# One 512-column matmul for the high and the low part of x in four stages of a two-block network

## The chip, the cores and the metric

The kernel runs on one core of one Trainium2 chip. The metric is the device time of one execution in microseconds (us). TensorE (PE in the profile) multiplies; VectorE (DVE), ScalarE (ACT) and GpSimd (POOL) work on vectors; SyncE (SP) issues the weight transfers. A difference is told apart from no change here when it is over 0.2%.

## The reference, cut to what matters

The program runs two blocks one after the other on x of 256 tokens by 2048 features, each block two layers deep.

```python
for i in range(DEPTH):                       # first block, layers 0 and 1
    h = rmsnorm(x, g_pre[i])
    u, z = split(h @ w_in[i])                # 4096 columns each
    y = pool_mixer(u, ...) if i == 0 else rglru(causal_depthwise_conv(u, ...), ...)
    y = y * silu(z)
    o = y @ w_out[i]
    x = x + rmsnorm(o, g_post[i])
    gate = sigmoid(rmsnorm(x, g_ple_in[i]) @ w_ple_gate[i])
    x = x + rmsnorm((p[i] @ w_ple[i]) * gate, g_ple_out[i])
for l in range(DEPTH):                       # second block, layers 2 and 3
    h = rms_norm(x, norm_g); proj = h @ w_in # attention, spatial gate and gated linear attention
    merged = g0 * (y_a @ w_branch[0]) + g1 * (y_b @ w_branch[1]) + g2 * (y_c @ w_branch[2])
    x = x + merged @ w_out
```

All of it is in float32.

## The kernel before

**Three products for one.** Each weight and each activation is kept as two fp32r numbers, a high part and a low part. A product is `w_hi*x_hi + w_hi*x_lo + w_lo*x_hi`; the term of both low parts is left out. Activations are stored as `[128, features/128, 512]` with the 256 tokens' high parts in columns 0 to 255 and their low parts in columns 256 to 511 (`xs`, `inner`, `latent`, `y_abc`, `merged`).

**Units.** Weights come as 1144 units of 8 tiles of 128x128. SP loads unit n into one of 4 slots of `raw`, ACT rounds it to `w_hi` (L1058), DVE subtracts to get `w_lo` (L1528), PE uses both. `LOOKAHEAD` is 3 units. A slot is free again when PE has finished the unit that was in it (`pe_mark`).

**Stages.** A stage is a number of turns over a few output tiles ("products") of a given depth. In the order of the program: window, pooled, silu, squared, plain, gate (layer 0); conv, lru, squared, plain, gate (layer 1); then for layers 2 and 3 gqk to za, twelve pairs mix_gate and mix_branch, and wo. The stages that this change speaks of are these:

- pooled: 4 turns of 8 products, depth 8 tiles, from `inner`; DVE takes each product out of its PSUM bank with bias and scale (L1971).
- silu: 8 turns of 4 products, depth 16, from `xs`; DVE multiplies with the norm's factor (L1978), ACT makes tanh (L1432), DVE finishes (L2050, L2056), POOL splits the result into `inner` (L2269, L2270).
- squared, in layers 0 and 1: 4 turns of 4 products, depth 32, from `inner`; ACT takes each product out twice, scaled (L1394) and squared (L1396), POOL adds the squares up (L2380).
- wo, in layers 2 and 3: 4 turns of 4 products, depth 16, from `merged`; DVE adds half of the product to `x_buf` (L2012).

In `products`, PE goes through a unit's 8 tiles twice: first two matmuls per tile with `w_hi`, on x's columns 0 to 255 (L591) and 256 to 511 (L592), both added into the same 256 columns of the bank, then one per tile with `w_lo` on columns 0 to 255 (L602). `first_turn` does the same for stages that go by rows of the weight matrix in their first turn (L732, L734, L754): here layer 1's squared and both wo. Each matmul loads its 128x128 stationary tile itself.

In the stages that go by token (gv, vb, uv, mix_gate, mix_branch; `token_products`), x is the stationary operand and the weights are the moving one, 512 columns at a time (L650 with `w_hi`, L667 with `w_lo`). There the moving operand is read through `four_runs`: runs of 4 numbers (16 bytes), each run 64 bytes after the last, 32 of them, and that four times over. The output is written straight through.

**What sets the order.** Every engine's instructions are in program order; semaphores tie them. PE waits for `hi_done` and `lo_done` of a unit, for the reader of what stood in a bank before (`occupant`, `read_of`), and in a stage's first turn for the tiles of its operand. pooled and silu rotate over 4 banks, squared over 7. ACT and DVE do a unit's split first and the evictions (`events`) of that unit after it. `SETTLED` and `settle` place pairs of 128-column matmuls (L612) whose result nothing reads. `xs_offset` is an unused buffer of 448 bytes that sets where `xs` and all behind it lie.

## Time and profile before

| | us |
|---|---|
| median of 3 runs | 3226.94 (3226.93 to 3227.39) |
| the profiled execution | 3227.28 |
| its span in the trace | 3225.4 |
| PE busy in the span | 3219.8 |
| DVE busy | 2248.8 |
| ACT busy | 1675.2 |

The span runs from the first to the last instruction of the trace; 1.9 us of the profiled execution lie outside of it. A matmul's "mean ns" in the trace is its latency, of which most lies under the matmuls before and after it; the time that one really takes of PE is the distance from start to start. The granted clock is 1.00 for the whole span.

### The profile page before, as it was taken

How to read it: one execution, taken by the hardware profiler on the slowest of the kernel's cores; microseconds unless marked ns; L12 is line 12 of the kernel's file. 1: busy time of each engine (PE TensorE's matmuls, PEld its weight loads, DVE VectorE, ACT ScalarE, POOL GpSimd, SP SyncE). 2: the span in 40 equal slices, each digit the busy share in tenths (PEclk: the TensorE clock that was granted, in tenths of full speed). 3: DMA queues.
4: the chain of work that ended last, by engine and by line, in shares of the span. 5: the costliest groups of instructions: out<-in, count | busy, mean ns of one | idle time of the engine just before them, and what ended most of it. 6: DMA issues, size and time to landing. Idle time of an engine off the chain costs nothing.

```text
span 3225.4 us, 57779 instructions
## 1 busy us (share of the span) xinstructions
PE 3219.8 (100%) x24078; PEld 3063.7 (95%) x24078; DVE 2248.8 (70%) x2898; ACT 1675.2 (52%) x2084; POOL 742.3 (23%) x782
## 2 busy tenths in 40 slices
PE   9999999999999999999999999999999999999999
PEld 9999999999999999999899988889999999888889
DVE  7986654588888844887889755555668897555554
ACT  5344444565588844655655544444455545444443
POOL 2632320054644400332523200000014332000000
PEclk9999999999999999999999999999999999999999
DMA  7565665556665665556455566666665554665665
GB/s 248 184 203 191 196 226 192 180 191 210 196 194 192 197 224 195 188 186 205 163 181 180 171 200 196 196 196 196 194 195 180 180 176 161 197 198 196 196 198 174
DMA packets 172596, 622.71 MB, mean 193 GB/s; under 512 B 19632, under 2 KB 22704, under 8 KB 171952
## 3 DMA queue, kind: packets, MB, share of 16 engines
q1 hardware_dynamic: 165888, 601.96, 57.5%
q10 hardware_dynamic: 6160, 16.02, 1.4%
q8 instruction: 190, 3.11, 0.4%
q0 software_dynamic: 288, 1.05, 0.1%
q14 instruction: 70, 0.57, 0.1%
HBM read 611.61 MB, written 5.24 MB: 191 GB/s over the span
## 4 chain that ended last, share of the span: by engine, by line
PE 99%; DVE 1%; DMA 0%; ACT 0%; issue 0%; ACTq 0%; DVEq 0%
PE banks L650 20%; PE banks L602 13%; PE banks L591 13%; PE banks L592 13%; PE banks L667 10%; PE pm L602 5%; PE pm L592 5%; PE pm L591 5%; PE banks L754 2%; PE banks L732 2%; PE banks L734 2%; PE pm L754 2%; PE pm L734 2%; PE pm L732 2%; PE pm L926 0%; PE pm L802 0%
## 5 line engine op out<-in xcount | busy, mean ns | idle before, releaser
L1528 DVE TENSOR_TENSOR w_lo<-raw,w_hi 128x1024 fp32r<-128x1024 f32 x1144 | 1471.0, 1291 | 855.6 <-ACT w_hi L1058 849.2
L1058 ACT ACTIVATE w_hi<-raw 128x1024 fp32r<-128x1024 f32 x1143 | 1203.8, 1058 | 1094.3 <-PE banks L667 460.2
L591 PE MATMUL banks<-xs,w_hi 128*128 128x256 f32 x2468 | 577.9, 277 | 0.2 <-DVE taps_in L2017 0.2
L592 PE MATMUL banks<-xs,w_hi 128*128 128x256 f32 x2468 | 576.6, 276 | 0.0
L650 PE MATMUL banks<-w_hi,xs 128*128 128x512 f32 x2048 | 493.5, 381 | 0.0
L591 PEld LDWEIGHTS banks<-xs,w_hi 128*128 128x128 f32 x2468 | 463.4, 188 | 0.7 <-DVE taps_in L2017 0.4
L592 PEld LDWEIGHTS banks<-xs,w_hi 128*128 128x128 f32 x2468 | 463.5, 188 | 0.3
L650 PEld LDWEIGHTS banks<-w_hi,xs 128*128 128x128 f32 x2048 | 383.8, 188 | 68.1
L602 PE MATMUL banks<-xs,w_lo 128*128 128x256 f32 x2468 | 338.1, 278 | 0.0
L602 PEld LDWEIGHTS banks<-xs,w_lo 128*128 128x128 f32 x2468 | 305.2, 188 | 3.6 <-issue 3.3
L667 PE MATMUL banks<-w_lo,xs 128*128 128x512 f32 x1024 | 270.6, 384 | 0.0
L591 PE MATMUL pm<-xs,w_hi 128*128 128x256 f32 x956 | 223.3, 276 | 0.0
L592 PE MATMUL pm<-xs,w_hi 128*128 128x256 f32 x956 | 223.3, 276 | 0.0
L667 PEld LDWEIGHTS banks<-w_lo,xs 128*128 128x128 f32 x1024 | 190.2, 188 | 32.6
L592 PE MATMUL banks<-inner,w_hi 128*128 128x256 f32 x896 | 211.0, 276 | 0.0
L591 PE MATMUL banks<-inner,w_hi 128*128 128x256 f32 x896 | 211.0, 276 | 0.0
L650 PE MATMUL banks<-w_hi,y_abc 128*128 128x512 f32 x768 | 184.3, 380 | 0.0
L591 PEld LDWEIGHTS pm<-xs,w_hi 128*128 128x128 f32 x956 | 179.5, 188 | 0.0
L592 PEld LDWEIGHTS pm<-xs,w_hi 128*128 128x128 f32 x956 | 179.5, 188 | 0.0
L592 PEld LDWEIGHTS banks<-inner,w_hi 128*128 128x128 f32 x896 | 168.2, 188 | 0.0
L591 PEld LDWEIGHTS banks<-inner,w_hi 128*128 128x128 f32 x896 | 168.2, 188 | 0.0
L650 PEld LDWEIGHTS banks<-w_hi,y_abc 128*128 128x128 f32 x768 | 144.1, 188 | 24.8
(411 smaller groups left out, 5428.6 us busy)
## 6 DMA issues: line engine op xcount, KB each, us to landing
raw<-weights SPq DMA_DIRECT2D x1143, 512.0 KB, 3.5
wide<-x_in ACTq DMA_DIRECT2D x1, 2048.0 KB, 8.7
x_scratch<-wide ACTq DMA_DIRECT2D x1, 2048.0 KB, 11.1
wide<-x_scratch ACTq DMA_DIRECT2D x1, 2048.0 KB, 8.9
wide<-x_in ACTq DMA_DIRECT2D x3, 512.0 KB, 6.8
out_x<-wide SPq DMA_DIRECT2D x3, 512.0 KB, 5.3
g_v<-x_scratch ACTq DMA_DIRECT2D x2, 512.0 KB, 4.9
w_st<-w_s ACTq DMA_DIRECT2D x2, 512.0 KB, 4.6
```

The lines of the kernel that those rows point to most:

```text
L591: nc.tensor.matmul(bank, w_hi[:, slot, w], x[:, 0:T], start=(k + t == 0), stop=False)
L592: nc.tensor.matmul(bank, w_hi[:, slot, w], x[:, T:2 * T], start=False, stop=False)
L602: ins = nc.tensor.matmul(bank, w_lo[:, slot, w], p.operand(i, k + t)[:, 0:T], start=False, stop=(k + t == p.depth - 1))
L650: nc.tensor.matmul(product_bank(s, i, j), x[:, at:at + P], four_runs(w_hi[:, slot, w]), start=(k == 0 and at < T), stop=False)
L667: ins = nc.tensor.matmul(product_bank(s, i, j), x[:, j * P:(j + 1) * P], four_runs(w_lo[:, slot, w]), start=False, stop=(k == depth - 1))
L732: nc.tensor.matmul(bank, w_hi[:, slot, w], operand[:, k, 0:T], start=(k == 0 and j < 4), stop=False, skip_group_check=True)
L734: nc.tensor.matmul(bank, w_hi[:, slot, w], operand[:, k, T:2 * T], start=False, stop=False, skip_group_check=True)
L754: ins = nc.tensor.matmul(bank, w_lo[:, slot, w], operand[:, k, 0:T], start=False, stop=(k == s.products[0].depth - 1), skip_group_check=True)
L1058: nc.scalar.activation(w_hi[:, slot, :], raw[:, slot, :], ACT.Copy).then_inc(hi_done, 1)
L1528: nc.vector.tensor_tensor(w_lo[:, slot, :], raw[:, slot, :], w_hi[:, slot, :].bitcast(F32), ALU.subtract).then_inc(lo_done, 1)
```

## The change

- In pooled, silu, the first 3 of squared's 4 turns, and all products of wo but the last (`wide`), one matmul with `w_hi` reads all 512 columns of x, so that the products with x's low part gather in columns 256 to 511 of the bank. It takes the place of the two 256-column ones.
- These matmuls read x and write the bank in the order that `in_runs` gives: runs of 4 numbers at a distance of 16, four times over. The `w_lo` matmuls of these products keep their 256 columns but go in the same kind of order.
- Whoever takes a product out adds the two halves. In pooled, silu and squared ACT copies columns 256 to 511 to one of two buffers `low_part` (in pooled with the scale and the bias, from `pool_shift`), and DVE adds that to columns 0 to 255. In silu DVE has a second instruction for the norm's factor. In squared DVE writes the sum to `whole`, and ACT makes its two outputs from there one unit later (`finish_wide`). In wo DVE has two chained instructions instead of one.
- `xs_offset` is 704 bytes instead of 448.

```diff
+    def wide(self, i, j):
+        if self.name == "squared":
+            return i < 3
+        if self.name == "wo":
+            return (i, j) != (3, 3)
+        return self.name in ("pooled", "silu")
...
+def in_runs(a, name):
+    return a.rearrange("p (g c f) -> p c g f", c=4, f=4)
...
-        sb("xs_offset", [P, 112])
+        sb("xs_offset", [P, 176])
...
+                            if s.wide(i, j):
+                                nc.tensor.matmul(in_runs(whole_bank(s, i, j), s.name), w_hi[:, slot, w], in_runs(x, s.name),
+                                                 start=(k + t == 0), stop=False, skip_group_check=True)
+                                continue
                             nc.tensor.matmul(bank, w_hi[:, slot, w], x[:, 0:T], start=(k + t == 0), stop=False)
                             nc.tensor.matmul(bank, w_hi[:, slot, w], x[:, T:2 * T], start=False, stop=False)
...
-                            ins = nc.tensor.matmul(bank, w_lo[:, slot, w], p.operand(i, k + t)[:, 0:T],
-                                                   start=False, stop=(k + t == p.depth - 1))
+                            ordered = in_runs if s.wide(i, j) else lambda a, name: a
+                            ins = nc.tensor.matmul(ordered(bank, s.name), w_lo[:, slot, w],
+                                                   ordered(p.operand(i, k + t)[:, 0:T], s.name),
+                                                   start=False, stop=(k + t == p.depth - 1),
+                                                   skip_group_check=s.wide(i, j))
...
+                def read_low_part(i, j):
+                    m = i * s.width + j
+                    sc.wait_ge(pe_mark, product_end(s, i, j))
+                    slot = len(low_parts) % 2
+                    if len(low_parts) >= 2:
+                        sc.wait_ge(*read_of(*low_parts[-2]))
+                    low_parts.append((s, i, j))
+                    part = whole_bank(s, i, j)[:, T:2 * T]
...
+                def finish_wide(i, j):
+                    m = i * s.width + j
+                    sc.wait_ge(*read_of(s, i, j))
+                    wait(sc, pool_done, m + (s.base["p"] - 3))
...
+                    elif s.name == "silu":
+                        ve.wait_ge(low_read, low_base + m + 1)
+                        link(nc.vector.tensor_tensor(v, product(s, i, j), low_part[:, (low_base + m) % 2, :], ALU.add))
+                        nc.vector.tensor_tensor(v, v, rstd_x[:], ALU.mult).then_inc(dve_read, 1)
+                    elif s.name == "squared":
...
+                        nc.vector.tensor_tensor(whole[:, j, :], product(s, i, j), low_part[:, (low_base + m) % 2, :], ALU.add)\
                             .then_inc(dve_read, 1)
```

PE in silu, the end of one unit's `w_hi` part, its `w_lo` part, and the start of the next, before (L591 and L592 are the two halves of x):

```order
L591 MATMUL banks<-xs,w_hi 128x256
L592 MATMUL banks<-xs,w_hi 128x256
L591 MATMUL banks<-xs,w_hi 128x256
L592 MATMUL banks<-xs,w_hi 128x256
L602 MATMUL banks<-xs,w_lo 128x256 x8
L591 MATMUL banks<-xs,w_hi 128x256
L592 MATMUL banks<-xs,w_hi 128x256
```

And PE in silu now, two whole units:

```order
L621 MATMUL banks<-xs,w_hi 128x4x32x4 x8
L636 MATMUL banks<-xs,w_lo 128x4x16x4 x8
L621 MATMUL banks<-xs,w_hi 128x4x32x4 x8
L636 MATMUL banks<-xs,w_lo 128x4x16x4 x8
```

Sixteen instructions of a unit's first part have become eight; the second part has as many as before.

DVE in silu over two units, which is one product, before:

```order
L1528 TENSOR_TENSOR w_lo<-raw,w_hi 128x1024
L1978 TENSOR_TENSOR val<-banks,rstd_x 128x256
L1528 TENSOR_TENSOR w_lo<-raw,w_hi 128x1024
L2050 SCALAR_TENSOR_TENSOR act<-act,val 128x256
L2056 SCALAR_TENSOR_TENSOR act<-act,wide 128x256
```

DVE at the same place now, with the semaphores that each waits for:

```order
L1609 TENSOR_TENSOR w_lo<-raw,w_hi 128x1024 [waits hi_done]
L2058 TENSOR_TENSOR val<-banks,low_part 128x256 [waits pe_mark,low_read]
L2059 TENSOR_TENSOR val<-val,rstd_x 128x256 [waits dve_chain]
L1609 TENSOR_TENSOR w_lo<-raw,w_hi 128x1024 [waits hi_done]
L2150 SCALAR_TENSOR_TENSOR act<-act,val 128x256 [waits act_ready]
L2156 SCALAR_TENSOR_TENSOR act<-act,wide 128x256 [waits dve_chain]
```

DVE's first instruction on a product now waits for ACT as well (`low_read`), and one instruction has come in behind it.

ACT at that place now (L1100 is what was L1058, L1542 the tanh that was L1432):

```order
L1533 ACTIVATE low_part<-banks 128x256 [waits dve_read,pe_mark]
L1100 ACTIVATE w_hi<-raw 128x1024 [waits pe_mark,raw_in1]
L1542 ACTIVATE act<-val 128x256 [waits pool_done,dve_read]
L1100 ACTIVATE w_hi<-raw 128x1024 [waits pe_mark,raw_in2]
```

ACT has a copy of the low half at the end of each product, and the tanh has moved behind the next unit's `w_hi` split.

## Rows read from the trace of the kernel before

**Rows 1.** The page, part 1: busy time of each engine, and PE's clock.

```profile
PE 3219.8 (100%) x24078; PEld 3063.7 (95%) x24078; DVE 2248.8 (70%) x2898; ACT 1675.2 (52%) x2084; POOL 742.3 (23%) x782
...
PEclk9999999999999999999999999999999999999999
```

**Rows 2.** The page, part 4: the chain of waits by engine.

```profile
PE 99%; DVE 1%; DMA 0%; ACT 0%; issue 0%; ACTq 0%; DVEq 0%
```

**Rows 3.** Waits of PE; columns: who waited for whom, us, times, longest.

```profile
PE pm L811 <- DVE g_o L1768: 1.0, 2, 0.5
PE pm L771 <- DVE mean_d L1894: 1.0, 1, 1.0
PE ms_bank L1033 <- DVE val L2081: 0.6, 2, 0.3
PE banks L591 <- DVE taps_in L2017: 0.2, 1, 0.2
```

**Rows 4.** Timeline of PE in silu; columns: start us, us, engine, line, form, count.

```profile
379.65 1.07 PE L602 MATMUL banks<-xs,w_lo 128*128 128x256 f32 x8
...
385.09 1.07 PE L602 MATMUL banks<-xs,w_lo 128*128 128x256 f32 x8
```

**Rows 5.** Timeline of PE in mix_gate.

```profile
1848.17 1.92 PE L650 MATMUL banks<-w_hi,xs 128*128 128x512 f32 x8
1849.93 1.04 PE L667 MATMUL banks<-w_lo,xs 128*128 128x512 f32 x4
1850.81 1.92 PE L650 MATMUL banks<-w_hi,xs 128*128 128x512 f32 x8
```

**Rows 6.** Groups of PE by line; after the bar: busy us, mean ns of one.

```profile
L650 PE MATMUL banks<-w_hi,xs 128*128 128x512 f32 x2048 | 493.5, 381 | 0.0
...
L667 PE MATMUL banks<-w_lo,xs 128*128 128x512 f32 x1024 | 270.6, 384 | 0.0
...
L592 PE MATMUL banks<-inner,w_hi 128*128 128x256 f32 x896 | 211.0, 276 | 0.0
...
L650 PE MATMUL banks<-w_hi,y_abc 128*128 128x512 f32 x768 | 184.3, 380 | 0.0
...
L667 PE MATMUL banks<-w_lo,y_abc 128*128 128x512 f32 x384 | 99.9, 380 | 0.0
...
L602 PE MATMUL banks<-latent,w_lo 128*128 128x256 f32 x160 | 25.4, 281 | 0.0
...
L667 PE MATMUL banks<-w_lo,latent 128*128 128x512 f32 x32 | 8.7, 393 | 0.0
```

**Rows 7.** Busy us (and count) by stretch: pooled, silu, squared of layers 0 and 1.

```profile
core 0: us, PE busy (x) PEld busy (x) DVE busy (x) ACT busy (x) POOL busy (x), PEclk, DMA share, GB/s
190.00:260.00 70.00, 70.00 (x620) 70.00 (x619) 49.92 (x75) 27.55 (x26) 0.00 (x0) 1.00 0.60 197
280.00:430.00 150.00, 150.00 (x1326) 150.00 (x1325) 99.57 (x137) 67.24 (x84) 56.71 (x55) 1.00 0.60 194
460.00:600.00 140.00, 140.00 (x1238) 140.00 (x1237) 63.70 (x54) 63.77 (x79) 9.65 (x13) 1.00 0.62 209
1130.00:1280.00 150.00, 150.00 (x1326) 150.00 (x1325) 68.43 (x58) 67.89 (x84) 11.03 (x14) 1.00 0.62 210
```

**Rows 8.** Groups by line of DVE and ACT in silu, 275 to 440 us, idle before and its releaser last.

```profile
L1528 DVE TENSOR_TENSOR w_lo<-raw,w_hi 128x1024 fp32r<-128x1024 f32 x61 | 74.9, 1228 | 44.7 <-ACT w_hi L1058 44.7
L1978 DVE TENSOR_TENSOR val<-banks,rstd_x 128x256 f32<-128x256 f32 x30 | 12.8, 425 | 10.1 <-PE banks L602 10.1
...
L1058 ACT ACTIVATE w_hi<-raw 128x1024 fp32r<-128x1024 f32 x61 | 64.3, 1054 | 28.8 <-PE banks L602 28.8
```

**Rows 9.** The eviction of DVE in pooled, by line, 184 to 266 us.

```profile
L1971 DVE TENSOR_SCALAR wide<-banks,chan 128x256 f32<-128x256 f32 x30 | 16.3, 543 | 8.0 <-PE banks L602 8.0
```

**Rows 10.** The same view for ACT in squared.

```profile
L1394 ACT ACTIVATE wide<-banks,chan 128x256 f32<-128x256 f32 x9 | 4.3, 475 | 14.1 <-PE banks L602 14.1
L1396 ACT ACTIVATE val<-banks 128x256 f32<-128x256 f32 x9 | 3.4, 378 | 0.0
```

**Rows 11.** Timeline of the end of the program.

```profile
3221.74 1.07 PE L602 MATMUL banks<-merged,w_lo 128*128 128x256 f32 x8
3222.85 0.42 DVE L2012 SCALAR_TENSOR_TENSOR wide<-banks,wide 128x256 f32<-128x256 f32 x1 [5.02 <-PE banks L602]
3223.30 0.33 SPq L553 DMA_DIRECT2D out_x<-wide  x1
```

**Rows 12.** Timeline of POOL at the end of silu.

```profile
445.25 1.42 POOL L2269 CAST inner<-act 128x256 fp32r<-128x256 f32 x1 [1.18 <-DVE act L2056]
446.75 0.75 POOL L2270 TENSOR_TENSOR inner<-act,inner 128x256 fp32r<-128x256 f32 x1
```

88 lines of the change are left out of this document (75 added, 13 removed).

## The prediction

> **What bounds the kernel now.** I read the page's busy times first, then the chain of waits, then PE's own waits, and only then the timelines. PE is busy for 3219.8 of 3225.4 us, at full clock in every slice [rows 1]; the chain that ended last is 99% PE [rows 2]; and all of PE's waits for others come to 1.0 + 1.0 + 0.6 + 0.2 = 2.8 us [rows 3]. So the time is the sum of the distances between PE's matmuls, and nothing else can give much. In the four stretches looked at, which lie in pooled, silu and both squared, PE has no idle time at all [rows 7]. DVE is busy for 71%, 66%, 46% and 46% of them, ACT for about 39% to 46% [rows 7].
>
> What one matmul costs PE must be read from starts, because its mean duration is latency (276 ns) that lies under its neighbours. In silu two units lie between the L602 rows at 379.65 and 385.09 us: 5.44 us for 2 x 24 matmuls of 256 columns, 113.3 ns each [rows 4]. In mix_gate one unit lies between 1848.17 and 1850.81 us: 2.64 us for 8 + 4 matmuls of 512 columns, 220.0 ns each [rows 5]. The two forms differ by 256 columns and 106.7 ns, which is 0.417 ns per column, the 2.4 GHz level. What is left is the same for both: 113.3 - 106.7 = 6.7 ns per matmul, whatever its width. That fixed part is the whole price at stake.
>
> **What the change removes on PE.** A wide tile had two `w_hi` matmuls, 226.7 ns; it now has one of 512 columns, 220.0 ns: 6.67 ns less. The `w_lo` matmul stays, at 113.3 ns. The tiles: pooled 32 products x 8 = 256; silu 32 x 16 = 512; squared, 12 products x 32 x 2 layers = 768; wo, 15 x 16 x 2 = 480; in all 2016. 2016 x 6.67 ns = 13.4 us. The unit in silu should fall from 2.72 to 8 x 0.2200 + 8 x 0.1133 = 2.667 us.
>
> The Trainium skill (TensorE: Matmul & The Clock Gate, section "Wait — 56ns, not 53.3ns?") gives a fixed cost of about 2.5 ns per matmul, not 6.7. By it, as an estimate, the saving would be 2016 x 2.5 ns = 5.0 us. The trace disagrees: the difference between the forms in rows 4 and 5 leaves 6.7, and the measurement decides.
>
> **Whether the new form costs what the old 512-column one costs.** Three things differ from mix_gate. First, x is the moving operand, not the weights; the reading order is the same runs of 4, and that order costs nothing in rows 5. Second, the bank is written in runs as well, which no row shows. Third, the `w_lo` matmul reads and writes 256 columns in runs, which no row shows either. The bounds: from below, no less than the columns alone, 213.3 and 106.7 ns, which would save another 13.4 us on the first and as much on the second; nothing in the trace comes near. From above, the dearest group of a matmul read in runs is L667 on `latent`, 393 against 380 ns on `y_abc`, 13 ns more, and of a 256-column one L602 on `latent`, 281 against 276, 5 ns more [rows 6]. 2016 x 13 = 26.2 and 2016 x 5 = 10.1 us. I take zero for both, since the big groups (x768 and x384 on `y_abc` at 380, x896 on `inner` at 276) stand at the low end and PE's distances in the steady stretches are one and the same number.
>
> **Where the two halves are added.** Pooled: ACT gains a copy per unit, by the nearest row 0.475 us [rows 10], and DVE's L1971, 543 ns [rows 9], becomes another instruction on one bank of about 0.43 us. Silu: per product ACT gains 0.475 us and DVE a second instruction of 0.43 us [rows 8, 10]. 32 of these are 14 us of DVE in silu's 174 us, which takes it from 66% to 75%. Squared: ACT reads PSUM once and SBUF twice where it read PSUM twice, 0.4 us more per product, and DVE gains 0.43. Wo: DVE gains 0.43 per product. None of it stands on PE's path. What hides it is that both engines wait for PE and not the reverse: ACT's split of a unit is held up by PE's release of a slot (28.8 us of idle in silu), and DVE's by ACT (44.7 us) [rows 8]. Queued behind ACT's new copy, which waits for the product's end, is the next unit's `w_hi` split, and behind DVE's wait for `low_read` the next `w_lo` split. Both are done three units, about 8 us, before PE needs them, so a delay of about 0.5 us per unit is absorbed. A bank's reader is half a microsecond later too; with four banks PE comes back to one after three units in pooled, after six in silu. If that cover were gone it would cost at most the copy itself per unit in pooled and per product in silu: 64 x 0.475 = 30 us.
>
> The longest hand-over is silu's last product into squared. POOL ends the last split at 447.5 us [rows 12], and PE needs that tile as the 32nd of squared's first product, nearly four units (10.5 us) after silu's last matmul, at about 453.6 us. A copy and one more vector instruction put the end of the split at about 448.5. It stays hidden.
>
> **The end.** The last product of wo is not wide, so what lies behind the last matmul (eviction at 3222.85, then the transfer at 3223.30 [rows 11]) is as it was: zero.
>
> **The shift by 256 bytes.** It changes how x's and the weights' addresses stand to each other in 12,832 matmuls of 256 columns and the 4,320 by token, too. What rows there are of the same form on differently placed buffers: 384 and 381 ns on `xs` against 380 on `y_abc` [rows 6]. If the shift brought `xs` to 380 it would give 1024 x 4 + 2048 x 1 ns = 6.1 us; if it brought all 12,832 contiguous ones from 276 to `latent`'s 281 it would cost 64 us. I take zero.
>
> **Sum.** The profiled execution of 3227.28 us (span 3225.4 and 1.9 around it) less 13.4 gives 3213.8 and a span of 3212.0; the median of the runs, 3226.94, is 0.3 lower, so 3213.5 us.
>
> **Rivals.**
>
> *Part of the saving is eaten* (0.14). The runs cost some 3 ns per tile over the wide and the `w_lo` matmul together, less than a quarter of the bounds above: 2016 x 3 = 6 us, so 3219.6, with 0.08 of this case below 3220.5 and 0.06 above. Merging two instructions could also save less than the whole fixed part, if some of it goes with the columns; half of it lost would be the same 6 to 7 us. For it: two forms out of three are new. Against it: 220.0 ns for 512 columns leaves no room for a part that grows with them. The skill's 2.5 ns (the page and section named above) would land in this case, at 3226.9 - 5.0 = 3221.9; rows 4 and 5 speak against it.
>
> *The shift helps the rest* (0.06): 3213.5 - 6.1 = 3207.4.
>
> *Nothing moves* (0.04): 512 columns of x are worked off as two passes of 256 and pay twice. Against it: rows 5, where 512 columns pay once. 3226.9.
>
> *PE waits for the adders* (0.03): the 30 us above, 3243.5. Against it: the idle times of rows 8.
>
> *Writing the bank in runs is slow* (0.08), the one by which it gets slower. If each jump from one run of 4 to the next cost one column's time, 0.417 ns, that would be 128 x 0.417 = 53 ns for a wide matmul and 27 ns for its `w_lo` one: 2016 x 80 = 161 us, so 3213.5 + 161 = 3375 us. It decides from 6.7 ns per tile on, which is one lost column in every 12 of a tile's 192 jumps. For it: the old kernel writes every one of its big matmuls straight through, also where it reads in runs. Against it: only that a run of 4 reads for free. The Trainium skill (PSUM — Partial Sum Buffer, section "Specifications (TRN2)") says that a non-contiguous access pattern slows matmuls significantly, with lines of 8 bytes. A run of 16 bytes fills two such lines whole, so the rule may not bite; no run here shows it yet.
>
> **How the numbers follow.** The forecast, 3213.5 us, has 0.65, with a range of its own of 3211 to 3217. A measurement here tells 0.2%, 6.5 us, from no change: faster is below 3220.5, slower above 3233.4. Faster: 0.65 + 0.06 + 0.08 (of the 0.14) = 0.79. Same: 0.06 + 0.04 = 0.10. Slower: 0.08 + 0.03 = 0.11. The range for 8 in 10 takes in the gain from the shift and the eaten saving: 3207 to 3223. It leaves out both slower cases and the dearer part of nothing moving.
>
> **What would show it.** In silu, pooled and squared the starts of the `w_lo` groups of following units 2.667 us apart, not 2.72 (so 16 units in 42.7 instead of 43.5 us); a wide matmul's mean near 380 ns and its `w_lo` one at 276; PE without idle time in these stages and no new releaser among its waits; gate, conv, lru and the stages by token as long as before. Wrong would be: a unit of 2.70 or more there (runs cost something), PE waits on `banks` with DVE or ACT as releaser (the adders), or stages without wide products that changed their length (the shift).

## The result, and the profile after

| | before | after |
|---|---|---|
| median of 11 runs each, same chip | 3227.39 us | 3235.78 us |
| span of the profiled execution | 3225.4 | 3234.3 |
| matmuls | 24078 | 22062 |

The change makes the kernel slower: ratio 1.0025, 95% interval 1.0017 to 1.0034. The forecast was 3213.5 us.

Part 1 and the clock of the page, and its chain by engine, after:

```profile
PE 3227.9 (100%) x22062; PEld 2990.6 (92%) x22062; DVE 2281.9 (71%) x2985; ACT 1709.4 (53%) x2172; POOL 750.2 (23%) x782
...
PEclk9999999999999999999999999999999999999999
...
PE 98%; DVE 1%; DMA 0%; ACT 0%; issue 0%; ACTq 0%
```

PE has 2016 matmuls less than in [rows 1], as counted, and is busy for 8.1 us more. It still bounds the kernel, at full clock. PE's waits after (who waited for whom: us in total, times, longest) hold nothing of the adders:

```profile
PE pm L813 <- DVE mean_d L1975: 1.0, 1, 1.0
PE pm L853 <- DVE g_o L1849: 1.0, 2, 0.5
PE ms_bank L1075 <- DVE val L2181: 0.6, 2, 0.3
PE banks L795 <- DVE w_lo L1609: 0.5, 1, 0.5
PE banks L772 <- ACT w_hi L1100: 0.4, 1, 0.4
```

Only the last two are new against [rows 3], 0.9 us together; both fall into window's first units, before any wide product. Busy time by stretch (pooled, silu, squared of layers 0 and 1; columns as in [rows 7]) shows PE full, with 867 matmuls in 150 us of silu where [rows 7] have 1326, and DVE at 73% there:

```profile
190.00:260.00 70.00, 70.00 (x416) 62.16 (x415) 49.15 (x75) 39.00 (x52) 0.00 (x0) 1.00 0.60 196
285.00:435.00 150.00, 150.00 (x867) 131.28 (x866) 109.96 (x163) 75.86 (x108) 58.74 (x55) 1.00 0.58 190
465.00:605.00 140.00, 140.00 (x887) 125.71 (x886) 67.67 (x64) 65.50 (x88) 12.27 (x13) 1.00 0.61 208
1135.00:1285.00 150.00, 150.00 (x972) 136.85 (x971) 72.94 (x69) 71.23 (x96) 12.98 (x14) 1.00 0.62 209
```

So the matmuls themselves take longer. Below, a unit's pace is the time from the start of its `w_lo` part to that of the next unit's; a unit is wide when its `w_hi` matmuls read 512 columns, and narrow otherwise. The timeline of PE at silu's start, after (start us, us, engine, line, form, count), answers to [rows 4]:

```profile
271.28 1.06 PE L636 MATMUL banks<-xs,w_lo 128*128 128x256 f32 x8
272.18 1.96 PE L621 MATMUL banks<-xs,w_hi 128*128 128x512 f32 x8
273.99 1.06 PE L636 MATMUL banks<-xs,w_lo 128*128 128x256 f32 x8
274.89 1.96 PE L621 MATMUL banks<-xs,w_hi 128*128 128x512 f32 x8
276.69 0.33 PE L648 MATMUL ms_bank<-xs,w_hi 128*128 128x128 f32 x2
276.86 1.14 PE L636 MATMUL banks<-xs,w_lo 128*128 128x256 f32 x8
```

And a hundred microseconds further on in silu:

```profile
382.27 1.11 PE L636 MATMUL banks<-xs,w_lo 128*128 128x256 f32 x8
383.23 2.01 PE L621 MATMUL banks<-xs,w_hi 128*128 128x512 f32 x8
385.07 1.07 PE L636 MATMUL banks<-xs,w_lo 128*128 128x256 f32 x8
385.98 2.00 PE L621 MATMUL banks<-xs,w_hi 128*128 128x512 f32 x8
387.82 1.11 PE L636 MATMUL banks<-xs,w_lo 128*128 128x256 f32 x8
```

At silu's start a unit takes 273.99 - 271.28 = 2.71 us, of which 274.89 - 273.99 = 0.90 are its eight `w_lo` matmuls and 1.81 its eight wide ones: 226 ns each, not 220.0. Then comes the settle pair (L648, two matmuls of 128 columns whose result nothing reads), and the units alternate between 2.80 and 2.75 us to the end of silu: dearer than the old 2.72 with eight matmuls more. The kernel before has its pairs at the same four places, where each costs 0.24 us once, and goes on at 2.720 after them.

The time of each stage, from the start of its first `w_lo` part to that of the next stage's, in us; the last two columns are kernels of the next section:

| stage (units) | before | after | after, without settle pairs | and `w_hi` moved, in layer 2's wo too |
|---|---|---|---|---|
| window (64) | 175.45 | 176.67 | 175.51 | 175.22 |
| pooled (32) | 87.28 | 86.96 | 87.04 | 86.21 |
| silu (64) | 174.32 | 177.55 | 174.08 | 172.37 |
| squared, layer 0 (64) | 172.96 | 175.45 | 172.75 | 171.50 |
| conv (64) | 174.41 | 174.06 | 174.03 | 174.80 |
| squared, layer 1 (64) | 172.96 | 174.31 | 172.76 | 171.52 |
| wo, layer 2 (32) | 87.93 | 87.93 | 87.93 | 87.18 |
| gqk, layer 3 (16) | 44.36 | 45.80 | 45.80 | 44.36 |

All other stages differ by at most 0.1 us before and after. The differences after - before in the table add up to 9.1 us, the span's is 8.9. Of it silu, the two squared and gqk make 8.5. Window and conv have no wide product and moved between -0.5 and +2.2 us from one profiled execution to the next in the runs below that leave them as they are, so nothing is read from them.

In layer 1's squared it is the last turn, which is not wide, that costs the time. Two of its units, after:

```profile
1280.47 1.11 PE L636 MATMUL banks<-inner,w_lo 128*128 128x256 f32 x8
...
1283.30 1.10 PE L636 MATMUL banks<-inner,w_lo 128*128 128x256 f32 x8
```

2.83 us, with 24 matmuls of the old form as in the 2.72 us of [rows 4]. gqk has no wide product either, and takes 45.80 us in every profiled kernel below that leaves layer 2's wo as it is here. PE there, after, shows two groups one unit apart:

```profile
2329.77 0.40 PE L795 MATMUL banks<-xs,w_lo 128*128 128x256 f32 x2
...
2332.59 0.40 PE L795 MATMUL banks<-xs,w_lo 128*128 128x256 f32 x2
```

And before:

```profile
2329.99 0.39 PE L754 MATMUL banks<-xs,w_lo 128*128 128x256 f32 x2
...
2332.71 0.39 PE L754 MATMUL banks<-xs,w_lo 128*128 128x256 f32 x2
```

2.82 against 2.72 us a unit, with the same instructions in the same order and, but for the 256 bytes of `xs_offset`, at the same places.

### The profile page after: what moved, and what is told of

Its sections match the earlier page's. It is cut to its first block, busy times and chain, and to the rows that moved or that the text cites. A ratio compares the mean times of both kernels' runs of the same rounds, so it can differ in the third digit from the quotient of the medians.

```text
span 3234.3 us, 54098 instructions
## 1 busy us (share of the span) xinstructions
PE 3227.9 (100%) x22062; PEld 2990.6 (92%) x22062; DVE 2281.9 (71%) x2985; ACT 1709.4 (53%) x2172; POOL 750.2 (23%) x782
## 4 chain that ended last, share of the span: by engine, by line
PE 98%; DVE 1%; DMA 0%; ACT 0%; issue 0%; ACTq 0%
PE banks L686 20%; PE banks L636 13%; PE banks L703 10%; PE banks L621 10%; PE banks L624 8%; PE banks L625 8%; PE pm L636 5%; PE pm L624 4%; PE pm L625 4%; PE pm L621 3%; PE banks L795 2%; PE pm L795 1%; PE banks L769 1%; PE banks L772 1%; PE banks L774 1%; PE pm L774 1%
## 5 line engine op out<-in xcount | busy, mean ns | idle before, releaser
L1100 ACT ACTIVATE w_hi<-raw 128x1024 fp32r<-128x1024 f32 x1143 | 1202.8, 1057 | 1042.0 <-PE banks L703 460.5
L624 PE MATMUL banks<-xs,w_hi 128*128 128x256 f32 x1956 | 458.7, 277 | 0.0
L625 PE MATMUL banks<-xs,w_hi 128*128 128x256 f32 x1956 | 457.5, 276 | 0.0
L624 PEld LDWEIGHTS banks<-xs,w_hi 128*128 128x128 f32 x1956 | 367.4, 188 | 0.3
L625 PEld LDWEIGHTS banks<-xs,w_hi 128*128 128x128 f32 x1956 | 367.4, 188 | 0.3
L621 PE MATMUL banks<-inner,w_hi 128*128 128x512 f32 x640 | 158.4, 388 | 0.0
L621 PEld LDWEIGHTS banks<-inner,w_hi 128*128 128x128 f32 x640 | 114.0, 187 | 19.3
L636 PE MATMUL pm<-xs,w_lo 128*128 128x256 f32 x956 | 129.7, 276 | 0.0
L636 PE MATMUL banks<-inner,w_lo 128*128 128x256 f32 x896 | 128.7, 276 | 0.0
```

Of the source, the lines that this page charges most:

```text
L621: nc.tensor.matmul(in_runs(whole_bank(s, i, j), s.name), w_hi[:, slot, w], in_runs(x, s.name), start=(k + t == 0), stop=False, skip_group_ ...
L624: nc.tensor.matmul(bank, w_hi[:, slot, w], x[:, 0:T], start=(k + t == 0), stop=False)
L625: nc.tensor.matmul(bank, w_hi[:, slot, w], x[:, T:2 * T], start=False, stop=False)
L636: ins = nc.tensor.matmul(ordered(bank, s.name), w_lo[:, slot, w], ordered(p.operand(i, k + t)[:, 0:T], s.name), start=False, stop=(k + t = ...
L1100: nc.scalar.activation(w_hi[:, slot, :], raw[:, slot, :], ACT.Copy).then_inc(hi_done, 1)
```

## The experiments

The first diff is against the kernel before, the next three are against the kernel after; all are cut to what matters. Where a result has two times, the second is the kernel before, run on the same chip. Of runs of one execution the trace is read, more than the time. The runs that read x from other places, exchange operands, or write straight after reading in runs compute something else; only their timing counts.

**The shift alone, and the change without it.**

```diff
-        sb("xs_offset", [P, 112])      # in the kernel before
+        sb("xs_offset", [P, 176])
```

> The kernel before with nothing but the 256 bytes more in xs_offset. In the trace of the changed kernel two stages without a single wide product have become longer: window by 1.22 us (its first turn) and layer 3's gqk by 1.44 us. Theory S (place: what a matmul costs depends on where x and the weights lie to each other) expects both here again, so +2.7 us and about 3230. Theory P (writing a bank in runs of 4 costs time) and theory X (reading x in runs of 4 costs time) say nothing on it: without S it stays at 3227.

3227.29 against 3227.53 us, ratio 1.000 (0.999 to 1.001); silu 174.32, both squared 172.96, as in the table to 0.01 us. And the other way round, 176 back to 112 in the kernel after:

> The changed kernel with xs_offset at its old 448 bytes. Theory S alone expects the wide matmuls at 220.0 ns instead of the mean of 228 that they have in the changed kernel, and the 2.7 us of window and gqk gone: 3213 to 3216 us. Theories P and X expect the wide matmuls to stay near 228 ns and only the 2.7 us to go: about 3233.

3236.93 us, ratio 1.0028 (1.0018 to 1.0038); silu 177.55, squared 175.45 and 174.31, gqk 45.80, as after. The 256 bytes do nothing, alone or with the rest.

**No runs.** Wide and `w_lo` matmuls read and write straight.

```diff
 def in_runs(a, name):
-    return a.rearrange("p (g c f) -> p c g f", c=4, f=4)
+    return a
```

> The changed kernel with in_runs giving its argument back: the wide matmul and its w_lo one read x and write the bank straight through, the place as in the changed kernel. Theories P and X expect 220.0 and 113.3 ns and a silu of 170.9 us (64 units of 2.667), in all 3213.5 + 2.7 = 3216. If it is the place alone (S) the wide matmuls stay above 220, and nothing says how far: the runs may as well be what keeps them low.

3241.23 us, ratio 1.0042 (1.0028 to 1.0056). A wide unit takes 2.773 us in every stage, before and (some four units on) after its pair; pooled 89.04. Two theories had expected 220.0 ns here and 3216 us in all. PE in silu, straight:

```profile
383.76 1.07 PE L636 MATMUL banks<-xs,w_lo 128*128 128x256 f32 x8
384.67 2.02 PE L621 MATMUL banks<-xs,w_hi 128*128 128x512 f32 x8
386.54 1.07 PE L636 MATMUL banks<-xs,w_lo 128*128 128x256 f32 x8
```

The wide ones now take 386.54 - 384.67 = 1.87 us, 233 ns each, the low ones 114. The runs are not the cause. They help in pooled, layer 1's squared and wo (2.707 or 2.720 us a unit); in silu behind its pair the average is 2.773 with them, too.

Layer 2's wo goes at 2.773 here as well, its last two, narrow units at 2.720, and gqk behind it is at 44.36 us again, with its own instructions untouched.

**Runs read, straight written.**

```diff
-    nc.tensor.matmul(in_runs(whole_bank(s, i, j), s.name), w_hi[:, slot, w], in_runs(x, s.name),
+    nc.tensor.matmul(whole_bank(s, i, j), w_hi[:, slot, w], in_runs(x, s.name),
...
-    ins = nc.tensor.matmul(ordered(bank, s.name), w_lo[:, slot, w],
+    ins = nc.tensor.matmul(bank, w_lo[:, slot, w],
```

> The changed kernel, reading x in runs as it does, but writing the bank straight through in the wide stages. The tokens then stand in another order and the two halves are mixed, so this is for the time of PE alone. Theory P expects 220.0 ns for a wide matmul, silu at 170.9 us and a total near 3216. Theories X and S expect silu to stay at 177.6 us and the total at 3236.

3237.35 us in one execution; pooled 86.96, silu 177.55, squared 175.45 and 174.30, as after to 0.01 us. How the bank is written costs nothing here. The Trainium skill (PSUM — Partial Sum Buffer, section "Specifications (TRN2)") says that a non-contiguous pattern there slows matmuls significantly; for runs of 16 bytes this pair of traces disagrees, 177.55 us of silu in both.

**No settle pairs in the wide stages**, one each in pooled, silu and both squared. The later diffs are against this kernel where nothing else is said.

```diff
-                            settle(slot, n - 1, p.operand(i, k)[:, 0:P])
+                            if not s.wide(i, j):
+                                settle(slot, n - 1, p.operand(i, k)[:, 0:P])
```

> The changed kernel without the pairs of 128-column matmuls (settle) in the stages with wide products; the waits before them stay. In the changed kernel pooled goes at 2.720 us a unit until its pair and at 2.707 after it, silu comes in at 2.706 and goes at 2.773 on average after its pair in turn 0. Theory M (the same sequence of matmuls has several steady paces, and what stands in between picks one) expects that without the pairs pooled stays at 2.720, and silu and the first squared stay at the pace they are entered with: about 64 x 0.053 + 48 x 0.053 = 6 us less, near 3230. Theory C (each stage has one pace, set by its operands' places) expects silu at 177.4 us and squared at 175.3 as in the changed kernel, 3235.4.

3228.09 against 3227.76 us, ratio 1.0002 (0.9992 to 1.0011). PE in silu:

```profile
382.25 1.08 PE L637 MATMUL banks<-xs,w_lo 128*128 128x256 f32 x8
383.16 1.96 PE L621 MATMUL banks<-xs,w_hi 128*128 128x512 f32 x8
384.96 1.08 PE L637 MATMUL banks<-xs,w_lo 128*128 128x256 f32 x8
385.88 1.96 PE L621 MATMUL banks<-xs,w_hi 128*128 128x512 f32 x8
```

A unit takes 2.720 us in every wide stage but wo (2.707). What pooled, silu and both squared lost in the kernel after was the pairs' doing, as the theory of several steady paces (M) had it; one pace for each stage (C) is refuted. But the merge gains nothing either: 2.720 is the old unit to the digit. The 0.20 to 0.24 us a stage by which this kernel lies below the kernel before in the table are the pair that it no longer has, 0.24 us each. The kernel before without its pairs was not run. Eight wide matmuls take 384.96 - 383.16 = 1.80 us, 225.5 ns each. The starts of single ones follow in steps that go round between 220 and 233 ns (220, 224, 227, 233, 230). The pairs are not bad as such: layer 1's squared goes from 2.720 to 2.707 at its pair in the kernel after, pooled too, and silu from 2.706 to 2.773 on the average.

**Other extra matmuls than a pair**: one of 16 to 256 columns at every fourth unit.

```diff
+                        if c == 0 and (s.layer, s.name, i, u) in SWEEP:
+                            wide_ = SWEEP[s.layer, s.name, i, u]
+                            nc.tensor.matmul(ms_bank[:, T:T + wide_], w_hi[:, slot, (n - 1) * P:n * P],
+                                             p.operand(i, k)[:, 0:wide_], start=True, stop=True, ...)
```

> As the run without pairs, but every fourth unit of silu, of squared in layer 0 (turns 0 to 2) and of squared in layer 1 (turns 1 and 2) has one matmul more between its w_hi and its w_lo part, of another width each time: 16 to 256 columns in silu, 72 to 248 in the first squared, 128, 128, 208, 208, 64, 192, 224, 240 in the second. Theory M expects the units between them to take one of a few values (2.707, 2.720, 2.773 us) by the width, and if a pace of 8 x 0.2200 + 8 x 0.1133 = 2.667 us can be had at all, some width to bring it. Theory C expects the unit to be the same whatever the width.

3240.93 us in one execution. Units settle at 2.707, 2.720, 2.742 to 2.775, or an alternation of 2.797 and 2.749, depending on the width and on the pace before; never at 2.667. Only three units lie between two of the extra matmuls, so 2.742 to 2.775 need not be steady; 2.707, 2.720 and the alternation hold for whole stages elsewhere. So a stream of one and the same kind has several paces, and one matmul may switch it.

**Is it the mix of 512 and 256?** The `w_lo` matmuls of the kernel after (with its pairs) read 512 columns as well.

```diff
+                            whole_ = s.wide(i, j)
-                            ins = nc.tensor.matmul(ordered(bank, s.name), w_lo[:, slot, w],
-                                                   ordered(p.operand(i, k + t)[:, 0:T], s.name),
+                            ins = nc.tensor.matmul(ordered(whole_bank(s, i, j) if whole_ else bank, s.name), ...
+                                                   ordered(p.operand(i, k + t)[:, 0:2 * T if whole_ else T], s.name),
```

> The changed kernel with the w_lo matmuls of wide products on all 512 columns of x too (this adds the product of both low parts, which costs time and serves nothing else). All matmuls of these stages then have one width, as in the stages by token. Theory W (a 512-column matmul of x goes at 220.0 ns only in a row of its like; changing to 256 columns and back upsets the weight loads) expects 220.0 ns each, 3.520 us a unit, silu at 225 us. Theories C and M without W expect the mean of the wide matmuls to stay at 225 ns or above, 3.60 us a unit or more.

3456.16 us in one execution. PE in silu:

```profile
299.92 1.98 PE L637 MATMUL banks<-xs,w_lo 128*128 128x512 f32 x8
301.75 1.97 PE L621 MATMUL banks<-xs,w_hi 128*128 128x512 f32 x8
303.55 1.98 PE L637 MATMUL banks<-xs,w_lo 128*128 128x512 f32 x8
```

3.63 us for 16 matmuls, 227 ns each. 512 columns alone are not at 220 either: it isn't the mix. (3.627 us is 32 times 113.3 ns, the old price of 256 columns.)

**Other runs**, in the kernel after, with its pairs. Numbers per run and distance: pooled 4 at 8, silu 8 at 32, squared 4 at 32, wo 2 at 16.

```diff
-    return a.rearrange("p (g c f) -> p c g f", c=4, f=4)
+    c, f = {"pooled": (2, 4), "silu": (4, 8), "squared": (8, 4), "wo": (8, 2)}[name]
+    return a.rearrange("p (g c f) -> p c g f", c=c, f=f)
```

> The changed kernel with other runs: in pooled 4 numbers at a distance of 8, in silu 8 at 32, in squared 4 at 32, in wo 2 at 16. Straight through, every one of these stages went at 2.773 us a unit; with 4 at 16 they go at 2.707, 2.720 or 2.773. Theory R (the order of reading decides how often a read of x meets the load of the next weights) expects other paces in these stages, with 2 at 16 the worst, since then half a line is read at a time. Theory M alone expects the same three paces.

3409.24 us in one execution: units of 2.813, 2.78, 2.89 to 2.96, and in wo 5.240. PE in wo:

```profile
2400.96 1.97 PE L637 MATMUL banks<-merged,w_lo 128*128 128x256 f32 x8
2402.73 3.66 PE L622 MATMUL banks<-merged,w_hi 128*128 128x512 f32 x8
2406.20 1.97 PE L637 MATMUL banks<-merged,w_lo 128*128 128x256 f32 x8
```

(2406.20 - 2402.73) / 8 = 434 ns: in runs of 8 bytes a wide matmul costs nearly double. Here x is read and the bank is written in such runs, and this run doesn't tell which of the two costs it; the next one does for reading.

**x read from other places**, by turn: each matmul of the wide stages reads x some bytes further on.

```diff
+SHIFTS = {("silu", _n): _d for _n, _d in enumerate((0, 4, 8, 12, 16, 24, 32, 48))}      # in numbers of 4 bytes
+SHIFTS.update({("pooled", _n): _d for _n, _d in enumerate((1, 2, 3, 20))})
+SHIFTS.update({("squared", 1): 64, ("squared", 2): 112})
```

> The run without pairs went at 2.720 us a unit in all wide stages: 1.804 us for 8 wide matmuls (220, 224, 227, 233, 229 ns in turn) and 0.916 for 8 w_lo ones. This run is the same but for where the wide matmuls and their w_lo ones read x: each turn reads some numbers further on, into the next tile (the product is then of other data, and only the time counts). silu, turn by turn: 0, 16, 32, 48, 64, 96, 128, 192 bytes; pooled: 4, 8, 12, 80 bytes; squared, turns 1 and 2: 256 and 448 bytes. Theory S in its last form (a distance between x and the weights that is no multiple of 256 bytes matters) expects some turns at 2.667 us and others above 2.720. If the place of x is of no weight all turns with whole lines of 16 bytes stay at 2.720, and only pooled's first three, whose runs straddle a line, could be slower.

3295.95 us in one execution. Pooled first, 8 bytes on, with a unit of over 5 us:

```profile
236.42 3.77 PE L649 MATMUL banks<-inner,w_hi 128*128 128x512 f32 x8
239.99 2.02 PE L665 MATMUL banks<-inner,w_lo 128*128 128x256 f32 x8
```

3.57 us for eight: 446 ns, double, when a run lies across a 16-byte boundary; the bank is written as before, so this is the reading alone. The Trainium skill (SBUF — State Buffer, section "Specifications (TRN2)") has lines of 16 bytes and asks for two hits per line; 8 bytes on, a run of 4 numbers has two hits in each of its two lines, and the trace shows that it is not enough here. Then silu with x 16 bytes on:

```profile
363.10 1.07 PE L665 MATMUL banks<-xs,w_lo 128*128 128x256 f32 x8
364.01 1.93 PE L649 MATMUL banks<-xs,w_hi 128*128 128x512 f32 x8
365.78 1.07 PE L665 MATMUL banks<-xs,w_lo 128*128 128x256 f32 x8
```

2.68 us a unit, 1.77 for the wide ones: 221 ns. Here is the price that the prediction took for a wide matmul (220.0), though the unit stays above its 2.667. Silu's eight places, 0, 16, 32, 48, 64, 96, 128 and 192 bytes on, give 2.720, 2.680, 2.733, 2.745, 2.714, 2.720, 2.720, 2.760.

The place doesn't decide by itself. In squared of layer 0, entered at 2.707, 256 and 448 bytes both give 2.707; in squared of layer 1, entered at 2.720, the same places give 2.720 and 2.760. So a figure for a place is one that some stream took there, and another past may give another.

**Which data, which role, which bank?** By turn of silu: the same x tile for all; roles exchanged; every other matmul into another bank; the same stationary tile; in squared both operands from `inner`, or both from `w_hi`.

```diff
+    stat, mov, to = w_hi[:, slot, w], in_runs(x, s.name), whole_bank(s, i, j)
+    if v == "1": mov = in_runs(p.operand(i, k), s.name)
+    if v == "2": stat, mov = x[:, 0:P], in_runs(w_hi[:, slot, (t % 2) * 2 * T:(t % 2 + 1) * 2 * T], s.name)
+    if v == "3" and t % 2: to = ms_bank[:, :]
+    if v == "4": stat = w_hi[:, slot, 0:P]
+    if v == "5": stat = p.operand(i, (k + t + 1) % p.depth)[:, 0:P]
+    if v == "6": mov = in_runs(w_hi[:, slot, (t % 2) * 2 * T:(t % 2 + 1) * 2 * T], s.name)
```

> As the run without pairs, but the wide matmuls take other operands, two turns of silu each (the results are of no use, and only the time counts): turns 0 and 1 the same x tile as moving operand for all 8 matmuls of a unit; 2 and 3 the roles swapped, x's first 128 columns stationary and 512 columns of w_hi moving, as in the stages by token; 4 and 5 every second matmul into another bank; 6 and 7 the same stationary tile for all 8. Squared: turn 1 both operands from inner, turn 2 both from w_hi. The stages by token pay 220.0 ns and silu 225.5 on average for the same number of columns, the same order of reading and the same line width. Theory B (which buffer is moving decides) expects 220 ns in the swapped turns and in squared's turn 2. Theory N (a matmul pays more when the moving tile is a new one each time; by token four in a row read the same) expects 220 in turns 0 and 1. Theory A (adding into the same bank without a pause) expects 220 in turns 4 and 5. Theory L (the load of a new weight tile under way is what disturbs) expects 220 only in turns 6 and 7.

3232.06 us in one execution: 2.720, 2.730, 2.773, 2.773 in silu, 2.707 and 2.722 in squared. No role, tile or bank brings back 220 ns; only the place did. (From the third pair of turns on silu goes at 2.773, which is also a pace of the plain stream, so what other banks or one stationary tile do by themselves is not shown.)

**More places, and the other forms.**

```diff
+SHIFTS = {(0, "silu", _n): _d for _n, _d in enumerate((132, 68, 36, 20, 124, 116, 100, 4))}
+SHIFTS.update({(0, "squared", 1): 4, (0, "squared", 2): 68, (1, "squared", 1): 124, (1, "squared", 2): 20})
+SHIFTS.update({(1, "conv", _n + 2): _d for _n, _d in enumerate((4, 8, 16, 32, 68, 124))})
+SHIFTS.update({(0, "gate", 2): 12, (0, "gate", 3): 20, (1, "gate", 2): 36, (1, "gate", 3): 116})
```

> Moving x's reading place by 16 bytes took a unit of silu from 2.720 to 2.680 us, with most wide matmuls at 220 ns; 32, 48, 64 and 192 bytes gave 2.733, 2.745, 2.714 and 2.760. This run reads more places, without the pairs: silu by turns 528, 272, 144, 80, 496, 464, 400 and 16 bytes; squared, turns 1 and 2, in layer 0 16 and 272, in layer 1 496 and 80; 256-column matmuls that are not wide in conv's turns 2 to 7 at 16, 32, 64, 128, 272, 496 bytes and in gate's turns 2 and 3 at 48, 80, 144, 464; and by token x's stationary tiles in layer 2's mix_gate blocks 1 to 3 at 16, 80 and 272 bytes. Theory S expects 2.68 us at 16 bytes in squared too (that it is not silu's alone), and the same at 528 if the pattern of places repeats every 512 bytes. For the 256-column matmuls it has nothing that excludes a price: if they stay at 2.720 us a unit at 16 bytes, x can be moved as a whole; if they go to 2.827 it can't.

3244.02 us in one execution. Wide: 2.680 at 16, 272 and 528 bytes, in silu and in squared; 2.72 to 2.75 at 80, 144, 400, 464 and 496. Narrow units (conv): 2.720 at 0, and 2.827 to 2.880 at 16, 32, 64, 128, 272 and 496 bytes. PE in conv with x 16 bytes on:

```profile
775.10 1.12 PE L657 MATMUL banks<-xs,w_lo 128*128 128x256 f32 x8
777.96 1.12 PE L657 MATMUL banks<-xs,w_lo 128*128 128x256 f32 x8
```

By token, where x is the stationary operand: 2.640 at 0, 2.680 at 16 and 272, 2.753 at 80. Gate's narrow units take 2.80 to 2.85 at 48, 80, 144 and 464. The places tried repeat every 256 bytes, and each form has its own good one. The old buffers lie at the good one of the old forms. The 2.827 at 128 bytes is also a pace of narrow units at 0 (layer 1's squared above), so there the past may be the cause.

**All of x 16 bytes further from the weights**, in every stage.

```diff
-        w_hi = sb("w_hi", [P, SLOTS, UNIT], F32R)
-        w_lo = sb("w_lo", [P, SLOTS, UNIT], F32R)
+        w_all = sb("w_all", [P, 2 * SLOTS * UNIT + 8], F32R)
+        w_hi, w_lo = (w_all[:, 4 + h * SLOTS * UNIT:4 + (h + 1) * SLOTS * UNIT]
+                      .rearrange("p (s u) -> p s u", u=UNIT) for h in range(2))
```

> The changed kernel without the pairs in the wide stages, and with w_hi and w_lo 16 bytes and x and all behind it 32 bytes further on, so that x stands 16 bytes further from the weights than in the changed kernel. Nothing else differs, and the results stay right. Theory S expects 2.680 us a unit in pooled, silu and the wide part of squared and wo: 252 units x 0.040 = 10 us less than the run without pairs, 3218 us, if the stages without wide products hold their pace. If those go from 113.3 to 118 ns a matmul (as stretches of them do now after a pair or after wo), each of their some 590 units costs 0.1 us more, and the total would be up to 3270.

3295.30 us, ratio 1.0208 (1.0191 to 1.0225). Conv +6.2 us, lru +9.1, each mix +8.0. And silu, 174.51 us, is at 2.727 a unit, not 2.680: here the weights' own place has changed, too.

**Only the weights moved, only while a wide stage runs.** The slot of unit n gets a shift that grows by 240 bytes on entering the wide stages and by 16 on leaving them; ACT's split of a unit waits for one more unit where the shift has grown.

```diff
+        def w_hi(n, w=slice(0, UNIT)):
+            at = n % SLOTS * UNIT + shift[n]           # 64 per wide episode passed, + 60 inside one
+            return w_all[:, at + w.start:at + w.stop]
+        def free_of(n, s, i, u):
+            moved = SLOTS <= n < n_units and shift[n] > shift[n - LOOKAHEAD]
+            return used(s, i, u) if moved else used_before(s, i, u)
```

> The changed kernel without the settle pairs in its wide stages (as in the earlier run, 3228.1 us, every wide unit 2.720), and now the weights' buffers lie 240 bytes further on while pooled, silu and the first three turns of each squared run, and 256, then 496, then 512 bytes further outside of them (twice 256 bytes in all; everything behind lies where it was, modulo 256 bytes). So x is read 16 bytes (modulo 256) further from the weights in these 192 units and nowhere else. Nothing is left out of the computation. Theory D (the distance between what is read as moving operand and the stationary tile, modulo 256 bytes, sets the pace, whichever of the two is moved): each of these units takes 2.680 us as where x's place was moved, so the time is 3228.1 - 192 x 0.040 = about 3220.4 us, 0.998 of the kernel before. Rival X (it is x's own place in its 256 bytes that counts, not the distance): the units stay at 2.720 us and the time at about 3228. Rival H (the sums of what ran before decide, and a correct program has another history): units at 2.707 to 2.773, time 3226 to 3236.

3233.67 against 3228.01 us, ratio 1.0017 (1.0008 to 1.0026). Units of 2.727 in pooled, silu and squared, narrow ones of squared 2.827. With both wo too:

> As the run with the weights moved in pooled, silu and squared, and in both wo as well (all but their last two units each, 60 units, which took 2.707 us). Nothing is left out. Theory D: another 60 x 0.027 = 1.6 us less, about 3218.8 us, and the gated attention projection behind the first wo (gqk of layer 3) starts from another pace than 2.827 us a unit, 1.4 us less if it comes back to 2.72: 3217.4 us. Rival X: about 3228 us, nothing moved.

3233.94 us, 1.0018 (1.0009 to 1.0027). The distance from x to the weights was the one that gave 2.680, and it didn't: theory D, that this distance sets the pace, is refuted. Then only `w_hi` moved (`w_lo` without the 60):

> As the run with the weights moved in pooled, silu and squared, but only w_hi lies 240 bytes further on in them; w_lo stays at a multiple of 256 bytes. So the 512-column matmuls read x 16 bytes further from their weights and the 256-column ones of the same unit don't. Nothing is left out. Theory D with each matmul by itself: the wide matmuls go to 220 ns (8 of them 1.76 us) and the low ones keep theirs (0.916 us): 2.680 a unit, about 3220.4 us, equal to both moved. Rival S (the stream as a whole has one pace, and a change of distance inside a unit breaks it): units at 2.72 to 2.80, time at or above 3228 us.

3222.61 us in one execution; units of 2.693, narrow turns of squared 2.720. And only `w_lo` moved:

> As the run before this one, the other way round: w_lo lies 240 bytes further on in pooled, silu and squared, w_hi doesn't. Nothing is left out. Theory D with each matmul by itself: the wide matmuls keep 225.5 ns and the low ones at most win what they have over 110 ns (8 x 4 ns = 0.03 us): 2.69 to 2.72 a unit, 3222 to 3228 us. Rival S (one pace for the stream): units at 2.72 to 2.80, at or above 3228 us, and the same as with only w_hi moved.

3230.14 us in one execution; units of 2.707, narrow ones 2.827. The two halves of a unit don't add up: against 2.720, one alone gives -0.027, the other alone -0.013, both +0.007. (2.707 is also a pace of the stream with nothing moved.)

**`w_hi` moved, in layer 2's wo as well.** The diff is against the run with only `w_hi` moved.

```diff
                     if s.name == "wo":
-                        is_wide = is_wide
+                        is_wide = s.layer == 2 and (i < 3 or u < s.units - 2)
```

> As the run with only w_hi 240 bytes further on in pooled, silu and squared (one execution of 3222.6 us, wide units 2.693 us), and now in layer 2's wo as well, in all but its last two units. Nothing is left out. Theory M (each pair of places, and the form of each half of a unit, has a pace of its own, which the next stage takes over): wo's 29 wide units of steady pace go from 2.707 to 2.693, 0.4 us; its last two, narrow, come from the new pace and run at 2.720 instead of 2.827 as they do behind squared, 0.2 us; and gqk of layer 3 starts from 2.720 and not 2.827, 1.44 us. 3222.6 - 2.0 = about 3220.6 us, 0.998 of the kernel before. Rival R (gqk's pace comes from its own first units): 3222.0 us.

3221.96 against 3227.83 us, ratio 0.9981 (0.9972 to 0.9990), span 3219.3, 6.1 us below the kernel before's. It is clearly faster than the kernel after; against the kernel before, the interval leaves out 1, but 0.19% is just under the 0.2% from which a difference is told here. By stage, 1.0 of the 6.1 us are the four pairs that it lacks, and 0.027 us a unit is what moving `w_hi` gives. PE in silu, then at wo's last two units:

```profile
382.82 1.08 PE L662 MATMUL banks<-xs,w_all 128*128 128x256 f32 x8
383.74 1.94 PE L646 MATMUL banks<-xs,w_all 128*128 128x512 f32 x8
385.51 1.08 PE L662 MATMUL banks<-xs,w_all 128*128 128x256 f32 x8
...
2299.41 1.07 PE L662 MATMUL banks<-merged,w_all 128*128 128x256 f32 x8
2302.13 1.07 PE L662 MATMUL banks<-merged,w_all 128*128 128x256 f32 x8
```

385.51 - 382.82 = 2.69 us a unit; wo's narrow units take 2.72 instead of 2.827, and gqk is back at 44.36. That the pace is handed over from stage to stage is shown: gqk itself was not touched, here as in the kernel that reads and writes straight. That gqk's pace would come from its own first units (R) is refuted.

**The place of `w_hi` swept**, again from the run with only `w_hi` moved; x and `w_lo` are fixed.

```diff
+SWEEP = {(0, "pooled"): (0, 0, 0, 0), (0, "silu"): (4, 8, 12, 16, 24, 32, 48, 56), (1, "squared"): (20, 28, 44, 0)}
```

> The run with only w_hi moved, with its place swept: 0 in pooled; 16, 32, 48, 64, 96, 128, 192, 224 bytes further on in silu's eight turns; 240 in layer 0's squared; 80, 112, 176 in the three wide turns of layer 1's. w_lo and x stay where they were, modulo 256 bytes. Nothing is left out. Theory M: the places give different paces, as those of x did (2.680 to 2.760 us a unit): 0 bytes 2.720, 240 bytes 2.693 again; since a place of x 16 bytes on with the weights at 0 gave 2.680 and w_hi 16 bytes back gave 2.693, part of it is the distance and part the weights' own alignment, so multiples of 64 bytes should be better than their neighbours. Rival A (only whether w_hi is at a multiple of 256 bytes counts): all places but 0 give 2.693. The time as a whole lies between 3221 and 3232 us.

3229.68 us in one execution. By place in bytes: 0 2.720; 16 2.733; 32 2.713; 48 2.702; 64 2.787; 80 2.713; 96 2.720; 112 2.710; 128 2.707; 176 2.713; 192 2.707; 224 2.757; 240 2.693. PE at 64 bytes, the dearest:

```profile
342.20 1.11 PE L664 MATMUL banks<-xs,w_all 128*128 128x256 f32 x8
343.15 2.00 PE L648 MATMUL banks<-xs,w_all 128*128 128x512 f32 x8
344.98 1.11 PE L664 MATMUL banks<-xs,w_all 128*128 128x256 f32 x8
```

Each place was tried once, behind whatever pace the last one left. Neither rule holds: not that only 0 differs, and not that multiples of 64 are better.

## Why the prediction was wrong

- **What bounds the kernel**: right. PE is the whole path before and after.
- **What the change removes**: the count was right, 2016 matmuls. The price was not.
- **The price of the new form**, taken from mix_gate's 512 columns at 220.0 ns with zero for what is new: this step failed. At the old place it takes 225.5 ns without the pairs (1.80 us for eight), against 226.7 for the two that it replaces: 1.2 ns saved per tile instead of 6.67, and lost again in the low ones at 114.5 instead of 113.3. The unit stays at 2.720 us, and the 13.4 us of the sum are nothing. That the fixed part is paid once per instruction was an inference from two forms, each of which stood at a place that suits it. At x 16 bytes on it is 221 ns: the step's number exists, but only at another operand place.
- **The upper bound of the unknown cost** was drawn from latencies, 13 ns per wide matmul, and would have held the result; I took the value at the low end because most rows stood there. The rows of 512 columns were all of by-token matmuls.
- **The settle pairs** appear in no step. The prediction treated a matmul's price as a property of its form. The kernel after shows 2.707, 2.720 and, on the average, 2.773 us for wide units, and 2.720 and 2.827 for narrow ones, and the four pairs have most of the say in it: without them the time is 3228.09 instead of 3235.78, 7.7 us less (7.6 by the table), of which 1.0 is the pairs' own time, which the kernel before pays too. This is why the result is not just no gain but a loss. The 1.44 us of gqk are lost to wo's last, narrow units, whose 2.827 us it takes over; they are in both of these kernels.
- **The adders**: right. No wait of PE for `low_part`'s readers, DVE at 73% in silu where 75% were forecast.
- **The end, the 256 bytes**: right. From the start of the last `w_lo` part to the end of the span it is 3.7 us before and after, and the shift alone gives ratio 1.000.
- **Rivals**: "writing the bank in runs is slow" is refuted by the run that writes straight. "Nothing moves" gave the time of the kernel without pairs, 3226.9 against 3228.1, and its price, that of two 256-column matmuls, holds to the digit for the unit at the old place (2.720 us, and 3.627 with 512 columns throughout). Its mechanism, two passes that pay twice, doesn't fit 16 bytes on: there a 256-column matmul takes 2.860 / 24 = 119 ns, and a wide one 221, not 238. The forecast gave this rival 0.04, and "slower", 0.11, only through the runs and the adders. That it would get slower by a change of pace was no rival.

What stays open: why a place suits one form and not another, and why a pair or the stage before can switch the pace. Shown is that the place of x and that of the weights both matter in steps of 16 bytes, that it repeats with 256 bytes for x, and that neither their distance nor the weights' alignment alone sets it. It wasn't tried to run the kernel before without its pairs or with `w_hi` moved, so how much of the last gain needs the merge is not known; nor to move the halves of x apart, or to use a pair where it helps (pooled, layer 1's squared) together with the moved `w_hi`.

## What to carry to other kernels

Where PE is busy all the time, read what an instruction costs from the start-to-start distance in the very stream and at the very addresses where it will stand; a price taken from another stage holds only there. Look at the pace of a stage before and after each odd matmul, and at the pace with which it hands over to the next. If a merge saves less than counted, sweep the operands' places by 16 bytes, one operand at a time, before giving it up: here a kernel with the same merge takes 0.25% more or 0.19% less than the one before, by where `w_hi` lies and whether four pairs stand in it.

## What the runs showed of the hardware

- A steady stream of equal units has several paces: 2.707, 2.720 and 2.773 us for wide units, 2.720 and 2.827 (3.9% apart) for narrow ones. A pair of 128-column matmuls switches between them, to either side (2.720 to 2.707 in pooled, 2.706 to 2.773 in silu), and the pace lasts for dozens of units and across stages (gqk 44.36 or 45.80 us).
- 16 bytes can decide: 2.680 to 2.787 us a wide unit by the place of x or of `w_hi`, with a period of 256 bytes for x in the places tried; 0.08 to 0.16 us more for narrow units at every place of x tried but 0. The pace before counts as well (448 bytes on: 2.707 or 2.760).
- Reading in runs of 16 bytes at a distance of 64 is cheaper than straight at most paces (225.5 against 233 ns per wide matmul) and equal at the dearest, 2.773 us a unit. Reading runs that lie across a 16-byte boundary costs double (446 ns), reading and writing in runs of 8 bytes nearly so (434 ns). Writing in runs of 16 bytes costs nothing (silu 177.55 us either way).
